# Layer norm over channels in a two-block transformer kernel: cross-tile sums on VectorE, then one matmul each

## The reference, cut to what matters

```python
def layer_norm(x, g, b):
    mu = jnp.mean(xf, axis=-1, keepdims=True)
    var = jnp.mean(jnp.square(xf - mu), axis=-1, keepdims=True)
    y = (xf - mu) * lax.rsqrt(var + EPS)
    return y * g + b

def conformer_conv(a, conv_w, conv_b, norm_g, norm_b, w_o):
    gl = a[..., :1024] * sigmoid(a[..., 1024:])
    y = depthwise_conv_31(gl, conv_w) + conv_b
    y = silu(layer_norm(y, norm_g, norm_b))
    return y @ w_o
```

## Time and profile before

| | before |
|---|---|
| median of 3 runs | 2228.06 us |
| the profiled execution's own time | 2226.02 us |
| its span (first to last instruction) | 2224.2 us |
| mean granted TensorE clock | 0.985 |
| busy: TensorE / weight loads | 95% / 83% |
| busy: VectorE / ScalarE / GpSimd | 75% / 55% / 3% |

### The profile page before, as it was taken

The page is one execution under the profiler, slowest core; times in us unless marked ns, Lnnn a source line. Parts: engine busy times, 40 slices in busy tenths (PEclk is TensorE's granted clock), DMA queues, the critical chain, the costliest instruction groups (busy, mean ns, idle before and its releaser), DMA issues.

```text
span 2224.2 us, 30895 instructions
## 1 busy us (share of the span) xinstructions
PE 2113.8 (95%) x12005; PEld 1841.2 (83%) x12005; DVE 1666.3 (75%) x2501; ACT 1224.8 (55%) x1651; POOL 58.8 (3%) x112
## 2 busy tenths in 40 slices
PE   7999989998999999999999999989999999998997
PEld 6777779896887887988887788789878878877996
DVE  6676667777778987766687898675687789976555
ACT  5555654555566446555556644554555675454543
POOL 3000000000000000000000000000000000000000
PEclk9999999999999999999999999999999999998999
DMA  7545775667645445677654444556555544444663
GB/s 254 182 156 181 236 257 169 223 216 227 206 144 159 134 142 161 199 231 242 204 187 133 139 135 143 177 175 191 174 174 171 152 133 133 151 161 143 189 187 117
DMA packets 203809, 394.31 MB, mean 177 GB/s; under 512 B 14007, under 2 KB 16563, under 8 KB 203664
## 3 DMA queue, kind: packets, MB, share of 16 engines
q1 hardware_dynamic: 198368, 381.74, 54.7%
q0 software_dynamic: 5296, 10.60, 1.6%
HBM read 390.98 MB, written 1.30 MB: 176 GB/s over the span
## 4 chain that ended last, share of the span: by engine, by line
PE 79%; DVE 9%; ACT 6%; issue 3%; DMA 2%; DVEq 0%; ACTq 0%
PE gps L1060 14%; PE gps L1062 14%; PE gps L1061 14%; PE gps L1067 9%; PE gps L1069 9%; PE gps L1068 9%; DVE wlo L1862 3%; ACT whi L1376 2%; PE aps L1019 2%; PE aps L864 2%; PE aps L995 1%; DMA raw<-ada_w 1%; PE aps L1026 1%; DVE Yc L1705 1%; PE gps L1054 1%
## 5 line engine op out<-in xcount | busy, mean ns | idle before, releaser
L1862 DVE TENSOR_TENSOR wlo<-raw,whi 128x1024 fp32r<-128x1024 f32 (+1 forms) x728 | 873.4, 1213 | 402.1 <-ACT whi L1376 398.8
L1376 ACT ACTIVATE whi<-raw 128x1024 fp32r<-128x1024 f32 (+1 forms) x728 | 756.6, 1049 | 625.8 <-PE gps L1062 360.7
L1060 PE MATMUL gps<-whi,ohi 128*128 128x512 f32 x1624 | 651.9, 401 | 9.6 <-DVE olo L1733 4.9
L1062 PE MATMUL gps<-whi,olo 128*128 128x512 f32 x1624 | 634.4, 391 | 0.0
L1061 PE MATMUL gps<-wlo,ohi 128*128 128x512 f32 x1624 | 634.0, 390 | 0.0
L1067 PE MATMUL gps<-ohi,whi 128*128 128x256 f32 x1760 | 503.8, 286 | 0.6 <-issue 0.5
L1068 PE MATMUL gps<-olo,whi 128*128 128x256 f32 x1760 | 498.5, 283 | 0.0
L1069 PE MATMUL gps<-ohi,wlo 128*128 128x256 f32 x1760 | 498.4, 283 | 0.0
L1060 PEld LDWEIGHTS gps<-whi,ohi 128*128 128x128 f32 x1624 | 306.3, 189 | 77.3 <-issue 9.7
L1062 PEld LDWEIGHTS gps<-whi,olo 128*128 128x128 f32 x1624 | 305.5, 188 | 65.6
L1061 PEld LDWEIGHTS gps<-wlo,ohi 128*128 128x128 f32 x1624 | 306.1, 188 | 61.3
(11 more groups left out here) (286 smaller groups left out, 1624.1 us busy)
## 6 DMA issues: line engine op xcount, KB each, us to landing
raw<-w_in SPq DMA_DIRECT2D x232, 512.0 KB, 3.8
raw<-w_ff SPq DMA_DIRECT2D x192, 512.0 KB, 4.1
raw<-ada_w SPq DMA_DIRECT2D x96, 512.0 KB, 4.8
raw<-w_out SPq DMA_DIRECT2D x32, 512.0 KB, 4.4
raw<-w_attn_o SPq DMA_DIRECT2D x24, 512.0 KB, 3.3
raw<-w_gmlp_o SPq DMA_DIRECT2D x24, 512.0 KB, 3.3
raw<-w_conv_o SPq DMA_DIRECT2D x24, 512.0 KB, 4.2
raw<-w_gate SPq DMA_DIRECT2D x20, 512.0 KB, 4.4
```

What stands on the lines that cost most here:

```text
L1060: mm(om, ah, whi[:, q, i, :], start=first, stop=False)
L1062: t = mm(om, al, whi[:, q, i, :], start=False, stop=last)
L1376: A_(part(whi, jb, q), part(raw, jb, q), ACT.Copy).then_inc(hi_done[q], 1)
L1862: tt(part(wlo, jb, q), part(raw, jb, q), f32(part(whi, jb, q)), ALU.subtract).then_inc(lo_done[q], 1)
```

## The change

A new VectorE step `over_tiles` adds the eight channel tiles elementwise with one `tensor_reduce`. It reads the source as 256 columns by eight tiles, the tile index innermost, so successive elements are 256 f32 apart, and writes 128x256 into the last quarter of `PTb`. TensorE then needs one f32 matmul by `ones` for each sum. It waits for a new semaphore `ln_pre`. The waits on the convolution, on `diag_add` and on the squares move from TensorE to VectorE. The list of semaphores also loses six names that nothing used.

```diff
-            def ln_sum(p, src, b):
-                for k in range(KT):
-                    t = mm(aps[:, b, 0:S], ones[:], src[:, k * S:(k + 1) * S], start=k == 0, stop=k == KT - 1)
-                return t
+            def ln_sum(b):
+                return mm(aps[:, b, 0:S], ones[:], PTb[:, 3 * S:4 * S], start=True, stop=True)
 
             def ln_mu(p):
                 free(p)
-                wait(pe, ev("cv_done", None, 0, p.conv_after), ("dg_add", None, 0, p.n + 1))
-                ln_sum(p, Yc, 2).then_inc(sem["ln_mean"], 1)
+                wait(pe, ev("ln_pre", p, 2, 1))
+                ln_sum(2).then_inc(sem["ln_mean"], 1)
 
             def ln_var(p):
                 free(p)
-                wait(pe, ev("ln_sq", p.of))
-                ln_sum(p, RB, 3).then_inc(sem["ln_vs"], 1)
+                wait(pe, ev("ln_pre", p.of, 2, 2))
+                ln_sum(3).then_inc(sem["ln_vs"], 1)
...
+            def over_tiles(src):
+                return nc.vector.tensor_reduce(PTb[:, 3 * S:4 * S], src[:].rearrange("p (k s) -> p s k", k=KT), AX.X, ALU.add)
+
             def ln_mu(p):
+                wait(dve, ("cv_done", None, 0, p.conv_after), ("dg_add", None, 0, p.n + 1))
+                over_tiles(Yc).then_inc(sem["ln_pre"], 1)
                 wait(dve, ev("ln_mean", p))
...
             def ln_var(p):
+                wait(dve, ev("ln_sq", p.of))
+                over_tiles(RB).then_inc(sem["ln_pre"], 1)
                 wait(dve, ev("ln_vs", p))
```

More of the change, by code:

```diff
@@ L555, in make_plan @@
     return jobs, tail
-SEMS = """x_in m_in ctx_in pr_in pr_in2 c_in rb_in cst_in tables_in ident_ready ones_ready c4_zeroed glp_zeroed
-pp_pc pp_th pp_c4 pp_pe pp_cols pp_pe2 pp_cols2 tp_tab tp_pe tp_r tp_st bias_in0 bias_in1
+SEMS = """x_in m_in ctx_in pr_in pr_in2 c_in rb_in cst_in ident_ready ones_ready
+pp_pc pp_th pp_c4 pp_pe pp_cols pp_pe2 pp_cols2 tp_pe tp_r tp_st bias_in0 bias_in1
 pn_ss pn_xn t_pe t_hi t_lo
@@ L563 @@
 cp_done res_done cg_cp cg_v cg_t cg_s up_mul up_hi up_lo ad_cp ad_st fin_ss fin_x
-mf_in mf_sum mf_pe mf_c mf_r mf_st gb_in q_cp kv_cp gqk_in tab_done rq_done rk_done tq_pe tq_cp tk_pe tk_cp
+mf_in mf_sum mf_pe mf_c mf_r mf_st gb_in q_cp kv_cp gqk_in rq_done rk_done tq_pe tq_cp tk_pe tk_cp
 at_s at_nb at_p at_r at_pn at_tp at_pt at_pv at_hi at_lo
 ge_sq ge_z ge_t ge_out gl_a gl_th gl_o gn_ss gn_done sp_pe sp_done
-ln_mean ln_d ln_sq ln_vs ln_n ln_s ln_th ln_r ln_hi ln_lo ga_th br_out cv_first cv_done dg_ready dg_used dg_add ws_in ws_pe ws_cp
+ln_pre ln_mean ln_d ln_sq ln_vs ln_n ln_th ln_r ln_hi ln_lo ga_th br_out cv_first cv_done dg_ready dg_used dg_add ws_in ws_pe ws_cp
 r2_relu r2_sq r2_hi r2_lo ac_cp ac_add y_add y_sq y_cp po_x out_st
```

## The result

The changed kernel takes 2266.85 us (median of five runs, 2264.0 to 2269.51) against 2229.28 for the kernel before: ratio 1.017, 95% interval 1.0158 to 1.0183, so 1.7% slower. The forecast said 2258 with a range of 2247 to 2273. The direction and the waiting held. The cost of the reduce did not: the size missed by 9 us, outside the 2254 to 2261 that I gave the likeliest case for itself and nearer to rival A's 2271. Its profiled execution took 2264.0 us, span 2262.2, which is 38.0 us longer than the span before.

A forecast was written before the change was run, and what follows sets the result against it. TensorE, busy 95% of the span, was taken to bound the kernel. Losses of 9.9 us at the means, 5.4 at the variances and 15.2 from the clock sum to 30.5: 2258 us forecast, range 2247 to 2273.

The forecast's parts named there:

- the likeliest case: Whole kernel: reduce at 2.28 us, TensorE waiting, clock falling six times; 2258 us, own range 2254 to 2261, chance 60%.
- rival A: Reduce at the six sums: strided read costs two slots per element, 4.41 us each, kernel 2271 us; chance 26%.
- TensorE bounds the kernel and its waits count in full: Whole kernel: TensorE busy 95% of the span, 79% of the chain; time gained or lost there counts in full.
- The removed matmuls: At the six sums: 14 of 16 TensorE instructions go, 3.02 us per sum, 18.1 us in all.
- Cost of the reduce: VectorE's new reduce at each sum: 2048 elements per partition at the trace's rate, 2.28 us.
- Idle time at ln_mu: TensorE before the three means: idles 5.99, 6.50 and 6.47 us waiting for VectorE; losses together 9.9 us.
- Idle time at ln_var: TensorE before the three variances: idles 4.82 us each waiting for VectorE's reduce; losses together 5.4 us.
- It is not given back: Behind ln_var: TensorE's 1.66 us wait for line 1733 stays, so its delay passes through and nothing is absorbed.
- The clock: Behind the six new idle stretches: granted clock falls to 0.5, about 2.53 us lost each, 15.2 us together.
- Rival B: Behind the sums: the clock holds or slow stretches fall into slack, only 15.3 us remains, 2243 us; chance 8%.
- Rival C: Later in the kernel: some 30 us of waits for line 1448 shorten and absorb the stalls, 2228 us; chance 3%.
- Rival D: At the six sums: VectorE has the reduce ready when TensorE arrives, gaining 18.1 us, 2210 us; chance 3%.

The follow-up runs named there:

- e1: The changed kernel with the reduce reading its 2048 elements in memory order, so sums are of wrong elements: 2257.39 us, ratio 1.0148.
- e4: The kernel before, TensorE keeping its 16 instructions per sum but waiting for a two-column VectorE copy where the change has the reduce: 2258.09 us, ratio 1.0141.
- e3: The changed kernel with unused matmuls in front of TensorE's waits, 32 at ln_mu and 26 at ln_var: 2251.48 us, ratio 1.0109.
- e5: The kernel before with only the mean moved to VectorE, as three contiguous adds early in branch3's first quarter; variance stays on TensorE: 2226.43 us, ratio 0.9996.
- e6: The kernel before, layer norm untouched, with unused matmuls in front of four transposes that wait for line 1448: 2222.53 us, ratio 0.9975.
- e2: The changed kernel with the reduce replaced by three contiguous adds of 1024, 512 and 256 columns: 2259.43 us, ratio 1.0143.

## Why the prediction was right in kind and short in size

- *TensorE bounds the kernel and its waits count in full.* Right: 36.1 of the 38.0 us are its idle time and its slow stretches at the six sums.
- *The removed matmuls.* Right, 12 instructions instead of 96.
- *Cost of the reduce, the step that was mis-sized.* I took 2.28 us, by rows that all read neighbouring elements, and it was 3.58. e1 gives 2.28 for the same instruction without the hop. In the sum that is 6 x 1.30 = 7.8 us, and 30.5 + 7.8 = 38.3 where 38.0 was measured. That this is so close is luck: the clock's term was 2.1 too large, and 1.9 us lie outside the account. The prediction's own sign, 3.5 to 4.4 in the reduce row, says rival A, which I gave 26%: the hop does cost, 1.57 times the contiguous read and not the two slots per element (4.41 us) that I priced. The Trainium skill, "Vector Engine (DVE) Microarchitecture Reference", section 5.2 "Measured stream behaviour on trn2", was the better guide: an estimate by its 1.73 ns per hopping element is 3.5 us plus the fixed part, and this trace agrees with 3.58. The same section's one-source op at full rate did not carry over to this one-source reduce. A measured figure for the access in question should have outweighed rows that don't show it.
- *Idle time at ln_mu.* Right but for the reduce: with 1.30 added, 5.99, 6.50 and 6.47 become 7.29, 7.80 and 7.77, measured 7.30, 7.82 and 7.82. The 3.9 to 4.4 us of them that no faster reduce can remove are what e4 shows.
- *Idle time at ln_var.* Forecast 4.82, with 1.30 it is 6.12, measured 6.06.
- *It is not given back.* Right; the wait behind it stayed at 1.64.
- *The clock.* Right in kind, six falls of six, and 13.1 us for a forecast 15.2. e3 shows it paid, 12.3 us over the mixers where 12.5 was due. Rival B falls with the after trace (the clock holds) and with e3 (slack). Rival C (taken up later) falls with the after trace too: the waits for line 1448 did not shrink.
- *Rival D, the gain.* For the mean its condition, VectorE ready before TensorE, was met by hand in the first mixer of e5 and nearly met in the others. Of the 9 us that D promises for the three means 3.2 were there (2.1, 0.5 and 0.5), since the chain behind the sums then makes TensorE wait. The variance's half was not tried.

The two errors, 7.8 too little and 2.1 too much, make 5.7 of the 7.5 us by which the profiled execution grew more than forecast (38.0 for 30.5), and the 1.9 us outside the account are the rest. The medians make it 9 because the change's profiled execution lay 2.9 us under its median, where the forecast had added 2.0, and by rounding.

## What to carry to other kernels

Before work moves from the bounding engine to one with spare time, look at what stands ahead of it in that engine's queue at that place: here a 0.16 us step at the same place costs 31 us. Then price the idle stretch that the hand-over makes on TensorE not only by its length but by the slow stretch behind it, about two microseconds each time in this kernel. And read the access pattern of the new instruction: a reduce over the outer index hops at every element, and adding halves contiguously does the same sum in 2.4 us for 3.6.

## What the runs showed of the hardware that I had not expected

- One idle stretch of 2.63 us was followed by a fall to 1.2 GHz and two of 2.64 us were not, in one execution (e4). Stretches of 3.88 us and more at the sums were followed by one every time. The trace of the kernel before could have told me: it has a fall behind 2.41 us, which the prediction, reading only stretches of 3.75 us and more and one of 1.66, passed over. The same stretch left the clock at 1.00 in e1 and e4. And e6 has a fall behind 1.97 us. The row of the stretch before and the window behind it:

```profile
179.46 0.47 PE L1060 MATMUL gps<-whi,ohi 128*128 128x512 f32 x1 [2.41 <-DVE olo L1562]
```

```profile
179.50:186.50 7.00, 7.00 (x24) 5.57 (x25) 4.72 (x4) 3.30 (x4) 0.00 (x0) 0.76 0.56 182
```

- The price of a fall varies between like places: windows behind the sums read 0.56 to 0.77, that is 3.1 to 1.6 us of 7. In the profiled execution of e1 the six add up to 14.5 us, in e2 to 15.1, and in the change, whose idle stretches are the longest of the three, to 13.1. One execution does not tell this term to a microsecond.
- The hopping reduce took 3.67 to 3.70 us beside e3's dense stream of unused matmuls, and 3.58 while TensorE idled. Which part they share, no run here shows. These are its rows in e3:

```profile
L1719 DVE TENSOR_REDUCE PTb<-Yc x3: 3665/3673/3697, 815.0 to 1962.5; 128x256 f32<-128x2048 f32 x3
L1719 DVE TENSOR_REDUCE PTb<-RB x3: 3698/3700/3700, 830.0 to 1977.4; 128x256 f32<-128x2048 f32 x3
```
